# GpSimd makes the keys' half of the span decays at five levels of the first block, VectorE keeps the queries' half

## The reference, cut to what matters

```
b = cumsum(g)                     # g: log forget gate, 4 heads x 64, per chunk of 64
diff  = b[:, :, :, None, :] - b[:, :, None, :, :]
decay = exp(where(t >= s, diff, -inf))
a = einsum('bhtd,bhsd,bhtsd->bhts', q, k, decay)
```

## Time and profile before

| | value |
|---|---|
| median of the runs | 1981.24 us |
| the profiled execution: its own time | 1981.44 us |
| the profiled execution: its span | 1979.6 us |
| TensorE matmul busy | 1963.1 us (99%) |
| VectorE busy | 1373.7 us (69%) |
| ScalarE busy | 1044.7 us (53%) |
| GpSimd busy | 37.1 us (2%) |
| mixing stage of the first block, layer 0: VectorE busy from 213 to 256 us | 41.52 of 43.00 us |
| same stretch of layer 1, from 697 to 740 us | 41.45 of 43.00 us |

### The profile page before, as it was taken

One profiled execution on the slowest core, in us unless ns is written; L12 is line 12 of the kernel. 1 busy time (PEld: TensorE's weight loads), 2 busy tenths in 40 slices (PEclk: granted clock), 3 DMA queues, 4 the chain that ended last, 5 costly groups with the idle time before them and its releaser, 6 DMA issues.

```text
span 1979.6 us, 26598 instructions
## 1 busy us (share of the span) xinstructions
PE 1963.1 (99%) x10822; PEld 1651.6 (83%) x10822; DVE 1373.7 (69%) x1684; ACT 1044.7 (53%) x1312; POOL 37.1 (2%) x73
## 2 busy tenths in 40 slices
PE   9999999999999999999999999999999999999998
PEld 8888988888888888888888898888888889888887
DVE  6666976666666696666666679766666667976665
ACT  5545575445444556544554466654454446675444
POOL 0120002000000000000000000000000000000000
PEclk9999999999999999999999999999999999999999
DMA  8765446665566454666566644356656664435662
GB/s 305 251 226 188 167 152 201 226 227 203 213 225 225 177 171 143 211 226 227 182 237 223 223 160 168 131 198 226 227 188 225 226 227 161 166 128 200 224 224 82
DMA packets 146603, 395.69 MB, mean 200 GB/s; under 512 B 82112, under 2 KB 100800, under 8 KB 104112
## 3 DMA queue, kind: packets, MB, share of 16 engines
q1 hardware_dynamic: 144560, 389.85, 56.6%
q0 software_dynamic: 1488, 3.78, 0.6%
q10 hardware_dynamic: 432, 0.35, 0.1%
HBM read 371.92 MB, written 19.66 MB: 198 GB/s over the span
## 4 chain that ended last, share of the span: by engine, by line
PE 84%; DVE 9%; ACT 4%; DVEq 1%; issue 1%; ACTq 0%
PE bank L458 79%; DVE w_lo L1358 4%; DVE arena L1496 1%; ACT w_hi L944 1%; PE bank L503 1%; PE bank L683 1%; DVE arena L1546 1%; PE bank L699 1%; PE bank L545 1%; DVE h_lo L1384 0%; DVEq L1576 0%; PE bank L783 0%; PE bank L764 0%; PE bank L802 0%; PE bank L626 0%
## 5 line engine op out<-in xcount | busy, mean ns | idle before, releaser
L1358 DVE TENSOR_TENSOR w_lo<-raw,w_hi 128x2048 fp32r<-128x2048 f32 x330 | 757.1, 2295 | 388.1 <-ACT w_hi L944 387.6
L944 ACT ACTIVATE w_hi<-raw 128x2048 fp32r<-128x2048 f32 x330 | 629.4, 1909 | 247.2 <-PE bank L458 244.9
L458 PE MATMUL bank<-w_hi,h_hi 128*128 128x512 f32 x1552 | 609.1, 392 | 1.5 <-DVE arena L1672 1.2
L458 PE MATMUL bank<-w_hi,h_lo 128*128 128x512 f32 x1552 | 604.7, 390 | 0.0
L458 PE MATMUL bank<-w_lo,h_hi 128*128 128x512 f32 x1552 | 604.5, 389 | 0.0
L458 PEld LDWEIGHTS bank<-w_hi,h_hi 128*128 128x128 f32 x1552 | 291.4, 188 | 64.8 <-DVE arena L1672 2.0
L458 PEld LDWEIGHTS bank<-w_hi,h_lo 128*128 128x128 f32 x1552 | 291.4, 188 | 61.2
L458 PEld LDWEIGHTS bank<-w_lo,h_hi 128*128 128x128 f32 x1552 | 291.5, 188 | 59.1
L458 PE MATMUL bank<-w_hi,act_hi 128*128 128x512 f32 x832 | 327.2, 393 | 3.3 <-DVE act_lo L1736 3.2
L458 PE MATMUL bank<-w_hi,act_lo 128*128 128x512 f32 x832 | 324.4, 390 | 0.0
L458 PE MATMUL bank<-w_lo,act_hi 128*128 128x512 f32 x832 | 324.1, 390 | 0.0
(11 more groups left out here) (236 smaller groups left out, 1367.5 us busy)
## 6 DMA issues: line engine op xcount, KB each, us to landing
raw<-stream SPq DMA_DIRECT2D x331, 1024.0 KB, 4.9
spill<-scratch SPq DMA_DIRECT2D x71, 256.0 KB, 3.6
scratch<-spill SPq DMA_DIRECT2D x71, 256.0 KB, 2.7
arena<-arena SPq DMA_DIRECT2D x32, 64.0 KB, 2.5
arena<-rpb POOLq DMA_DIRECT2D x16, 66.5 KB, 4.0
x<-xt SPq DMA_DIRECT2D x4, 256.0 KB, 5.7
raw<-stream SPq DMA_DIRECT2D x2, 512.0 KB, 6.1
arena<-final_gain POOLq DMA_DIRECT2D x2, 512.0 KB, 5.5
```

The costliest lines, as they stand in the source:

```text
L458: last = mm(o, a, r, start=start and n == 0, stop=stop and n == len(pairs) - 1)
L944: fn(w_hi[u % SLOTS][:, :], raw[u % RAW][:, :], ACT.Copy).then_inc(hi_done, 1)
L1358: tt(w_lo[u % SLOTS][:, :], raw[u % RAW][:, :], w_hi[u % SLOTS][:, :].bitcast(F32), ALU.subtract).then_inc(lo_done, 1)
```

## The change

In the first block, at levels 2 to 6 of `STEPS` (m = 16, 8, 4, 2, 1), GpSimd issues the two subtractions for the keys and VectorE the two for the queries. GpSimd waits until VectorE has finished `span_scale(t - 1)`, which is the last reader of `dec`. ScalarE's `span_exp(t)` waits for both engines. Level 1 (m = 32), the two levels beyond a chunk and the second block stay as they are. The helper `halves` moves to where both engines' programs can use it.

```
+POOL_STEPS = [2, 3, 4, 5, 6]
...
 # GpSimd, last in its loop over the layers of the first block
+                for t in POOL_STEPS:
+                    pool.wait_ge(qks_ready, len(STEPS) * layer_no(0, L) + t)
+                    f_lo, f_up = halves(cum[:, 0:2, :], STEPS[t])
+                    b_lo, b_up = halves(cum[:, 2:4, :], STEPS[t])
+                    k_lo, k_up = halves(dec[:, 2:4, :], STEPS[t])
+                    pool.tensor_tensor(k_lo, f_lo[:, :, STEPS[t] - 1:STEPS[t]].to_broadcast(tuple(k_lo.shape)), f_lo, ALU.subtract)
+                    pool.tensor_tensor(k_up, b_up, b_up[:, :, 0:1].to_broadcast(tuple(k_up.shape)), ALU.subtract).then_inc(key_decay_ready, 1)
...
 # ScalarE
             def span_exp(b, L, t):
                 act.wait_ge(d_ready, (len(STEPS) - 1) * layer_no(b, L) + t)
+                if b == 0 and t in POOL_STEPS:
+                    act.wait_ge(key_decay_ready, len(POOL_STEPS) * L + POOL_STEPS.index(t) + 1)
                 fn(dec[:, :, :], dec[:, :, :], ACT.Exp, scale=(1 / 16, 1.0)[b]).then_inc(e_ready, 1)
...
 # VectorE, span_decay
-                    less(halves(fq, m)[1], up, ref)
-                    ins = less(halves(fk, m)[0], ref, lo)
+                    ins = less(halves(fq, m)[1], up, ref)
+                    if b == 1 or t not in POOL_STEPS:
+                        ins = less(halves(fk, m)[0], ref, lo)
                     if b == 0:
                         lo, up = halves(bx, m)
                         ref = up[:, :, 0:1]
-                        less(halves(fq, m)[0], ref, lo)
-                        ins = less(halves(fk, m)[1], up, ref)
+                        ins = less(halves(fq, m)[0], ref, lo)
+                        if t not in POOL_STEPS:
+                            ins = less(halves(fk, m)[1], up, ref)
```

More of the change, by code:

```diff
@@ L222, in build @@
         sum_ready = sem("sum_ready")
-        slab_moved = sem("slab_moved")
+        slab_moved, key_decay_ready = sem("slab_moved"), sem("key_decay_ready")
         rows_ready, fox_ready = sem("rows_ready"), sem("fox_ready")
@@ L322, in head_bank, with halves @@
             return PB[1] if b == 1 and item >= LATE_ITEM else PD[3]
+        def halves(ap, m):
+            w = ap.rearrange("p c (n two m) -> p (c n) two m", two=2, m=m)
+            return w[:, :, 0, :], w[:, :, 1, :]
         block = ctx.enter_context(nc.Block())
@@ L1484, in ffn @@
                         split(use_of("down", g - 1) + SLOTS)
-            def halves(ap, m):
-                w = ap.rearrange("p c (n two m) -> p (c n) two m", two=2, m=m)
-                return w[:, :, 0, :], w[:, :, 1, :]
             def less(dst, a, r):
```

## The result

The changed kernel takes 1984.3 us (median of 20 runs) against 1981.36 us for the kernel before: 0.15% slower, ratio 1.0015 with a 95% interval of 1.0009 to 1.0021. The profiled execution took 1984.02 us, its span is 1981.9 us. The forecast was 1985.5 us, range 1978.7 to 1989.5. The direction was right and the loss is 2.9 us instead of 4.3, but it came about in another way than forecast.

The account below looks back on a forecast made before the run. TensorE's matmuls fill 99% of the span, and VectorE's unbroken chain from 220 to 256 us feeds it. The profiled 1981.44 us + 4.3 for two layers = 1985.7, less 0.2 for the median: 1985.5 us, range 1978.7 to 1989.5.

Parts of the forecast that it names:

- the two stalls named: TensorE waits at 224.66 us for an eviction queued behind VectorE's decays (0.76 us) and at 247.96 for the softmax's division.
- 0.67 us a level to be saved: VectorE issues two decays instead of four before the split, 0.67 us less; five levels in two layers make 6.7 us.
- The gain that was put at 2.5 us: Rival without costly collision: TensorE loses its stalls up to 256 us, 1.25 us a layer, 1978.7 us; chance 0.22.
- the 0.4 us at 247.96: Part of the no-collision gain: about 0.4 us of TensorE's stall before the softmax's division goes in each layer.
- The two engines exclude each other: A VectorE instruction with two SBUF operands and a GpSimd one don't run together; a GpSimd addition took 2.47 us, not 0.42.
- VectorE first: After L1546, VectorE issues two decays and the split before GpSimd starts: +4.3 us in two layers, 1985.5 us; chance 0.38.
- Rival 1: GpSimd starts first, VectorE's first decay stands still for both subtractions, lasting some 1.6 us: +5.2 us, 1986.4; chance 0.25.
- The one that waits doesn't get in between: GpSimd, waiting, cannot enter between VectorE's back-to-back decays and split, so it starts only when the split is over.
- taking turns: With GpSimd first, the engines alternate by single instructions: 1.89 us to the split, +0.46 a level, +4.6 in all, 1985.8.
- The size of GpSimd's read: A GpSimd subtraction of 128 x 256 was estimated at 0.56 us of reading, 1.23 us for a pair; bounds 0.84 and 1.7.
- Rival 3: GpSimd is much slower with short inner runs, a pair taking 1.7 us or more: +9 us, 1990.5; chance 0.09.
- one long wait for the division: TensorE gets the softmax's probabilities at 250.1 us instead of 247.96, 2.15 us lost a layer, +4.3 in two.

Follow-up runs that it names:

- keys left out: Changed kernel without the keys' decays of levels 2 to 6 on either engine and without ScalarE's wait for GpSimd: 1978.91 us against 1981.23, ratio 0.9989.
- the early keys: Changed kernel with first-block span decays moved to other memory, so GpSimd can make a level's keys earlier, beside VectorE's PSUM reads: 1979.59 us against 1981.17, ratio 0.9992.
- the fills: Changed kernel with each of GpSimd's subtractions replaced by a memset of the same size, which writes but does not read: 1979.12 us against 1981.23, ratio 0.9990.
- the doubled kernel: Changed kernel with GpSimd making each subtraction twice, once into memory nobody reads, four instructions a level: 1995.83 us against 1980.95, ratio 1.0076.
- The order that was forecast, forced: Changed kernel with GpSimd waiting by a semaphore until VectorE has finished its own two decays of the level: 1986.4 us against 1981.23, ratio 1.0028.

## Why the prediction came out as it did

- **What bounds the kernel: right.** VectorE is on the chain from 220 to 256 us and hands every delay to TensorE; the two stalls named are those that grew, and those that went when GpSimd's work was left out. 0.67 us a level to be saved: measured with the keys left out. The gain that was put at 2.5 us was 3.1 at TensorE; of its three terms, the 0.4 us at 247.96 was 0.64.
- **The two engines exclude each other: right, and the decisive step.** The rows of a 2.47 us addition and a 3.71 us split were enough to see it. That operands from PSUM don't count was assumed, and the early keys showed it; that it is GpSimd's reading and not its writing which excludes, the prediction had not told apart, and the fills showed it.
- **VectorE first: wrong.** GpSimd starts 0.08 us after its release and VectorE's decay 0.09 us after, so GpSimd is first by 0.01 us in all ten levels. I took the handover from a DMA issue, 0.29 us; arithmetic is handed over in 0.08, nearer to ScalarE's 0.03. Rival 1 is what happened.
- **"The one that waits doesn't get in between": wrong, and the step that the forecast's loss hung on.** In the changed kernel GpSimd's second subtraction, begun at 220.82 during VectorE's first decay, is served before the second decay; in the doubled kernel the third is served between the last decay and the split. So even with VectorE first by 0.2 us, GpSimd would by these rows have got its turn after the first decay, and the split would have begun as late as it does now: two decays and two subtractions stand ahead of it in either order. That case was not run. The forecast's chain appears only where GpSimd is released when the split has begun.
- **Within rival 1, turns and not a block.** I had put 2.6 us a layer on "the first decay stands still for both" and 2.3 on taking turns, and had held the 3.7 us split against taking turns. The changed and the doubled kernel show turns. In the changed kernel the first decay takes 0.88 us, not the 1.6 that I named as rival 1's sign.
- **The size of GpSimd's read: too long.** 0.56 us estimated, 0.44 measured. Taking turns then costs 0.22 us a level, since 2 x 0.44 is only 0.2 above the 0.67 us that VectorE saves; with 0.56 it was 0.46. This term alone takes the 4.6 us of taking turns to 2.1, and 2.0 were seen. Short runs cost GpSimd nothing: a pair takes the same at every level. Rival 3 falls.
- **What was missing:** 0.7 us from the place of VectorE's instructions, which no view of the kernel before could have given.
- **The number: near by luck.** The forecast had +4.3 us from one long wait for the division, at about 250 us. What happened is 2.0 us from turns, 0.7 from the pauses and a collision near 320 us that can go either way. The order that was forecast, forced, costs 5.2. One sum is off as well: with 1.7 us for a pair the forecast's chain gives +4.0 us a layer, not +4.2, which lowers the upper bound by 0.3 us.
- **The chances.** 0.15% slower lies inside the 0.2% that I called no change. The interval of the twenty runs, 0.09 to 0.21%, shows the loss all the same.

## What to carry to other kernels

Moving elementwise work from VectorE to GpSimd paid here only in moments when VectorE read at most one operand from SBUF: beside evictions from PSUM, it was free; beside VectorE's own instructions with two operands in SBUF each GpSimd instruction that reads costs VectorE its whole reading time, here 0.44 us. When the two take turns, what matters is what runs at the moment at which GpSimd is released: behind a short decay it waits 0.2 us, behind a split that has begun 2 us. An edit that shortens an engine's program can move costs in code that it never touches, so an unexplained few tenths of a microsecond far from the edit should be tested with padding before it is explained.

## What the runs showed of the hardware that I had not expected

- GpSimd's subtraction of 128 x 256 takes 0.61 us alone and follows the last at 0.57 us, of which 0.44 us exclude VectorE; its fill of the same size takes 0.31 us and excludes nothing.
- A GpSimd instruction starts 0.06 us (a fill) or 0.08 us (a subtraction) after the VectorE instruction that releases it, though one of its DMA issues came 0.29 us after the activation that released it.
- GpSimd and VectorE alternate by single instructions when both read SBUF; the exception, a split that waits for several of GpSimd's additions, is in five traces of thirteen.
- Pauses of 0.35 us in VectorE's stream that ten drains a layer, hundreds of microseconds earlier, take away.
- TensorE's granted clock fell to a mean of 0.56 to 0.59 for 4 us after a stretch of 4 us in which it was busy for 2.0; at the same place of layer 1, busy for 2.1 of 4 us, it stayed at 1.00. In the doubled kernel, where the wait is 3.9 us in both layers, it fell in both: to 0.50 from 254 to 258 us, and to 0.55 to 0.60 from 744 to 748 us. Why the shorter wait does it once and not twice is open.
